# K's inverse norms to rows through DRAM from head 2 on, and K's squares turned inside Q's product

## The reference

```
x = x + pool_mixer(rmsnorm(x));  x = x + mlp(rmsnorm(x))        # layer 0; mlp: square(relu(h @ w_in)) @ w_out, width 4096
kv = rmsnorm(x) @ w_kv                                          # (512, 2048): K for 8 heads x 2 halves of 64, V for 8 heads of 128
k  = rmsnorm(kv[..., :1024] per group of 64) * k_norm
q  = rmsnorm((rmsnorm(x) @ w_q) per group of 64) * q_norm / 8
s  = q @ k.T + bias(distance bucket, head), causal               # two score matrices per head
a  = softmax(s[0]) - lambda * softmax(s[1]);  o = a @ v
x = x + (rmsnorm(o per head) * subln * (1 - lambda_init)) @ w_o;  x = x + mlp(rmsnorm(x))
```

## Time and profile before

| | us |
|---|---|
| median of 3 runs (lowest, highest) | 941.27 (940.96, 941.45) |
| the profiled execution's own time | 941.54 |
| its span | 939.7 |
| PE busy | 934.1 (99%) |
| DVE busy | 683.8 (73%) |
| ACT busy | 470.7 (50%) |
| POOL busy | 89.8 (10%) |
| granted clock of TensorE | 1.0 |

### The profile page before, as it was taken

How to read it: one execution, slowest core, us unless ns; L and a number is a source line. 1 busy time by engine, 2 the same in 40 slices (tenths; PEclk the granted TensorE clock), 3 DMA queues, 4 the chain that set the end, 5 groups by cost and what they waited for, 6 DMA issues and landing times.

```text
span 939.7 us, 11721 instructions
## 1 busy us (share of the span) xinstructions
PE 934.1 (99%) x4439; PEld 771.6 (82%) x4439; DVE 683.8 (73%) x989; ACT 470.7 (50%) x614; POOL 89.8 (10%) x70
## 2 busy tenths in 40 slices
PE   9999999999999999999999999999999999999998
PEld 7888888888888888888888887888888888888887
DVE  6876766676676689988887886757766676667685
ACT  7644343333434438787777773535334333433441
POOL 3000000100000002123222220000100000010010
PEclk9999999999999999999999999999999999999999
DMA  7328682494556644233333232336485458248535
GB/s 258 105 90 239 153 234 90 99 264 129 135 142 173 179 85 120 71 107 93 102 103 103 90 101 90 90 91 188 126 248 155 122 121 250 90 92 225 175 90 135
DMA packets 101583, 130.45 MB, mean 139 GB/s; under 512 B 4297, under 2 KB 63481, under 8 KB 101537
## 3 DMA queue, kind: packets, MB, share of 16 engines
q1 hardware_dynamic: 85632, 98.31, 32.0%
q0 software_dynamic: 14080, 29.91, 17.5%
q10 hardware_dynamic: 1824, 1.61, 0.7%
HBM read 127.69 MB, written 4.75 MB: 141 GB/s over the span
## 4 chain that ended last, share of the span: by engine, by line
PE 91%; DVE 4%; ACT 2%; DMA 2%; issue 1%; SPq 0%; ACTq 0%; DVEq 0%
PE bank L1695 28%; PE bank L1697 28%; PE bank L1696 28%; PE bank L1967 2%; PE bank L1957 1%; DMA raw<-in_w_mlp_out_dram 1%; DVE w_low L1080 1%; PE bank L1996 1%; DMA work<-in_x_dram 1%; PE bank L1872 1%; DVE a_low_buf L1163 0%; ACT w_high L729 0%; ACT w_high L666 0%; PE bank L1938 0%; PE bank L1806 0%
## 5 line engine op out<-in xcount | busy, mean ns | idle before, releaser
L1695 PE MATMUL bank<-h_high_buf,w_high 128*128 128x512 f32 x640 | 252.2, 394 | 0.0
L1697 PE MATMUL bank<-h_high_buf,w_low 128*128 128x512 f32 x640 | 249.5, 390 | 0.0
L1696 PE MATMUL bank<-h_low_buf,w_high 128*128 128x512 f32 x640 | 249.1, 389 | 0.0
L1695 PE MATMUL bank<-w_high,a_high_buf 128*128 128x512 f32 (+1 forms) x452 | 176.1, 390 | 0.1
L1697 PE MATMUL bank<-w_high,a_low_buf 128*128 128x512 f32 (+1 forms) x452 | 175.1, 387 | 0.0
L1696 PE MATMUL bank<-w_low,a_high_buf 128*128 128x512 f32 (+1 forms) x452 | 175.1, 387 | 0.0
L1080 DVE TENSOR_TENSOR w_low<-raw,w_high 128x2048 fp32r<-128x2048 f32 (+2 forms) x56 | 120.3, 2148 | 51.4 <-ACT w_high L729 31.8
L1695 PEld LDWEIGHTS bank<-h_high_buf,w_high 128*128 128x128 f32 x640 | 120.2, 188 | 26.5 <-issue 2.2
L1697 PEld LDWEIGHTS bank<-h_high_buf,w_low 128*128 128x128 f32 x640 | 120.1, 188 | 25.5
L1696 PEld LDWEIGHTS bank<-h_low_buf,w_high 128*128 128x128 f32 x640 | 120.3, 188 | 24.1
L738 ACT ACTIVATE work<-work 128x512 f32<-128x512 f32 x64 | 40.0, 632 | 177.9 <-DVE work L1147 177.9
(11 more groups left out here) (187 smaller groups left out, 1162.5 us busy)
## 6 DMA issues: line engine op xcount, KB each, us to landing
raw<-in_w_mlp_out_dram SPq DMA_DIRECT2D x24, 1024.0 KB, 6.8
raw<-in_w_mlp_out_dram POOLq DMA_DIRECT2D x24, 1024.0 KB, 8.5
raw<-in_w_mlp_in_dram SPq DMA_DIRECT2D x16, 1024.0 KB, 6.2
work<-in_w_mlp_out_dram SPq DMA_DIRECT2D x8, 1024.0 KB, 5.1
work<-in_w_mlp_in_dram SPq DMA_DIRECT2D x8, 1024.0 KB, 7.6
raw<-in_w_kv_dram SPq DMA_DIRECT2D x16, 512.0 KB, 4.0
xT<-in_w_mlp_out_dram SPq DMA_DIRECT2D x8, 1024.0 KB, 4.8
xT<-in_w_mlp_in_dram SPq DMA_DIRECT2D x8, 1024.0 KB, 7.0
```

What stands on the lines that cost most here:

```text
L1695: pe.matmul(acc, w_hi, m_hi, start=start, stop=False, skip_group_check=onto)
L1696: pe.matmul(acc, w_hi, m_lo, start=False, stop=False, skip_group_check=onto)
L1697: return pe.matmul(acc, w_lo, m_hi, start=False, stop=stop, skip_group_check=onto)
```

## The change

From head 2 on (n = 2 to 7, prepared in heads 1 to 6) K's inverse norms no longer pass PE. K's sums get their own eps, root and inverse ahead of Q's (`k_sums`, `k_roots`, `k_inverses`), SP stores them to a DRAM tensor of two rows of 512 and reads each row back into 64 partitions of the buffer of K's squares (`spread_k_rows`), and `k_norm_rows` multiplies K with it at a stride of four. The spread by DVE and the turn by PE go for these heads. SP issues the store and the two loads between its loads of K's and Q's weights and its load of V's. `turn_ksq` moves from behind Q's product to behind five of its eight chunks. POOL waits for `k_inverse` before its K half split. Heads 0 and 1 are normalized as before.

```diff
--- before.py
+++ after.py
@@ -239,6 +239,7 @@
 
         SUM_BANK = [I[0], I[1], I[2], I[3], O[2], O[3], I[1], I[3]]
 
+        k_row = nc.dram_tensor("k_rstd_rows", (2, S), F32, kind="Internal").ap()
         o_row = nc.dram_tensor("o_rstd_row", (S,), F32, kind="Internal").ap()
         scratch_rows = nc.dram_tensor("bias_rows_by_distance", (H, REL), F32, kind="Internal").ap()
         scratch = nc.dram_tensor("bias_by_distance", (H, P, REL), F32, kind="Internal").ap()
@@ -283,6 +284,12 @@
         half_low = sem("half_low")
         pool_low = sem("pool_low")
         w_used = sem("w_used")
+
+        k_total = sem("k_total")
+        k_rooted = sem("k_rooted")
+        k_inverse = sem("k_inverse")
+        k_row_stored = sem("k_row_stored")
+        k_row_landed = sem("k_row_landed")
 
         consts_ready = sem("consts_ready")
         zeros_ready = sem("zeros_ready")
@@ -530,12 +537,32 @@
 
             load_mlp(0)
 
-            with sp.Fori(0, H) as n:
+            def load_kq(n):
                 slot_free(U_HEAD + 2 * n)
                 sp.dma_start(tile3(raw[1][:, 0:1024], KC), wk_v[:, :, bass.ds(n * P, P)]).then_inc(w_landed[1], 16)
                 sp.dma_start(tile3(raw[1][:, 1024:2048], KC), wq_v[:, :, bass.ds(n * P, P)]).then_inc(w_landed[1], 16)
+
+            def load_v(n):
                 slot_free(U_HEAD + 1 + 2 * n)
                 sp.dma_start(tile3(raw[0][:, 0:1024], KC), wk_v[:, :, bass.ds(D + n * P, P)]).then_inc(w_landed[0], 16)
+
+            def spread_k_rows(n):
+
+                sp.wait_ge(k_inverse, n - 1)
+                sp.dma_start(k_row.rearrange("c (p i) -> p c i", p=P), kq_rstd_buf[:, 0:8].rearrange("p (c i) -> p c i", c=2))\
+                  .then_inc(k_row_stored, 16)
+                sp.wait_ge(k_row_stored, 16 * n - 16)
+                sp.wait_ge(kn_ready, n)
+                for c in range(2):
+                    sp.dma_start(ksq[c * HD:(c + 1) * HD, :], k_row[c:c + 1, :].to_broadcast([HD, S])).then_inc(k_row_landed, 16)
+
+            with sp.Fori(0, 3) as n:
+                load_kq(n)
+                load_v(n)
+            with sp.Fori(3, H) as n:
+                load_kq(n)
+                spread_k_rows(n - 1)
+                load_v(n)
             for f in range(NF):
                 for q in range(2):
                     u = U_WO + 2 * f + q
@@ -547,6 +574,8 @@
                     else:
                         sp.dma_start(tile3(raw[u % 2], 4), wo_v[:, 4 * q:4 * q + 4, f * S:(f + 1) * S])\
                           .then_inc(w_landed[u % 2], 16)
+                    if u == U_WO:
+                        spread_k_rows(H - 1)
             load_mlp(1)
 
             for p, half, f in ((P2, 0, 0), (P3, 0, 1), (P7, 1, 1), (P4, 1, 0)):
@@ -647,6 +676,8 @@
                     pool.wait_ge(k_low_done, 1)
                 if h == 1:
                     pool.wait_ge(neg_ready, 2)
+                if h >= 2:
+                    pool.wait_ge(k_inverse, h - 1)
                 if h == H - 1:
                     pool.wait_ge(half_high, h + 1)
                     pool.tensor_tensor(w_low_buf[1][:, 0:UNIT // 2], raw[1][:, 0:UNIT // 2], w_high_buf[1][:, 0:UNIT // 2].bitcast(F32),
@@ -881,6 +912,15 @@
                 act.wait_ge(kq_total, n + 1)
                 act.activation(kq_root_buf[:, :], kq_sum_buf[:, :], ACT.Sqrt, scale=1.0 / HD).then_inc(kq_rooted, 1)
 
+            def k_roots(n):
+
+                act.wait_ge(k_total, n - 1)
+                act.activation(kq_root_buf[:, 0:8], kq_sum_buf[:, 0:8], ACT.Sqrt, scale=1.0 / HD).then_inc(k_rooted, 1)
+
+            def q_roots(n):
+                act.wait_ge(kq_total, n + 1)
+                act.activation(kq_root_buf[:, 8:16], kq_sum_buf[:, 8:16], ACT.Sqrt, scale=1.0 / HD).then_inc(kq_rooted, 1)
+
             def k_high(n):
                 act.wait_ge(kn_ready, n + 1)
                 act.activation(k_hi, kf, ACT.Copy).then_inc(k_high_done, 1)
@@ -1003,6 +1043,7 @@
                 split_v(n)
                 if not second:
                     split_high_first(n + 1, kq_landed(n + 1))
+                k_roots(n)
                 square_q(n)
                 q_high(n)
                 if second:
@@ -1010,7 +1051,7 @@
                 at_highs(h, range(1))
                 if last:
                     o_high(0)
-                kq_roots(n)
+                q_roots(n)
                 o_roots(h - 1)
                 at_highs(h, range(1, 3))
                 bias_scale(n, (0, 1))
@@ -1446,10 +1487,32 @@
                 if first:
                     dve.tensor_tensor(w_low_buf[0][:, 512:1024], raw[0][:, 512:1024], f32(w_high_buf[0][:, 512:1024]), ALU.subtract)\
                        .then_inc(w_low, 1)
-                else:
-                    q_low(n)
                 kq_reduce(n, q_bank, qsq_turned, 1)
                 kq_add_eps(n)
+
+            def k_sums(n, b):
+
+                kq_reduce(n, b, ksq_turned, 0)
+                dve.wait_ge(kq_sum, 2 * n + 1)
+                dve.tensor_tensor(kq_sum_buf[:, 0:8], kq_sum_buf[:, 0:8], kq_eps[:, :], ALU.add).then_inc(k_total, 1)
+
+            def q_sums(n, b):
+
+                kq_reduce(n, b, qsq_turned, 1)
+                dve.wait_ge(kq_sum, 2 * n + 2)
+                dve.tensor_tensor(kq_sum_buf[:, 8:16], kq_sum_buf[:, 8:16], kq_eps[:, :], ALU.add).then_inc(kq_total, 1)
+
+            def k_inverses(n):
+
+                dve.wait_ge(k_rooted, n - 1)
+                dve.reciprocal(kq_rstd_buf[:, 0:8].rearrange("p (c i) -> p i c", c=2), kq_root_buf[:, 0:8].rearrange("p (i c) -> p i c", c=2))\
+                   .then_inc(k_inverse, 1)
+
+            def q_inverses(n):
+                dve.wait_ge(kq_rooted, n + 1)
+                dve.reciprocal(kq_rstd_buf[:, 8:16], kq_root_buf[:, 8:16]).then_inc(kq_inverse, 1)
+                dve.wait_ge(kq_inverse, n + 1)
+                dve.tensor_scalar(neg_rstd_q[:, :], kq_rstd_buf[:, 8:16], -1.0, None, ALU.mult).then_inc(neg_ready, 1)
 
             def half_low_of(n):
                 dve.wait_ge(half_high, n)
@@ -1473,6 +1536,12 @@
             def k_norm(n, b):
                 dve.wait_ge(k_turned, n + 1)
                 dve.tensor_tensor(kf, kf, b[:, :], ALU.mult).then_inc(kn_ready, 1)
+
+            def k_norm_rows(n):
+
+                dve.wait_ge(k_row_landed, 32 * n - 32)
+                k = kf.rearrange("p (i n) -> p i n", i=TT)
+                dve.tensor_tensor(k, k, ksq.rearrange("p (n i) -> p i n", i=TT), ALU.mult).then_inc(kn_ready, 1)
 
             def k_low(n):
                 dve.wait_ge(k_high_done, n + 1)
@@ -1606,15 +1675,24 @@
                 combine(h, 3)
                 if not first:
                     split_low(U_HEAD + 1 + 2 * n, 0, 1024)
+                    k_sums(n, I[0])
                     o_sums(h - 1, I[3])
-                kq_sums(n, I[0], O[3], first)
-                kq_inverses(n)
+                    k_inverses(n)
+                    q_low(n)
+                    q_sums(n, O[3])
+                    q_inverses(n)
+                else:
+                    kq_sums(n, I[0], O[3], first)
+                    kq_inverses(n)
                 if not first:
                     if not second:
                         dve.wait_ge(o_row_stored, 16 * h - 16)
                     o_inverses(h - 1)
                 at_lows(h)
-                k_norm(n, I[0])
+                if first:
+                    k_norm(n, I[0])
+                else:
+                    k_norm_rows(n)
                 if first:
                     q_low(n)
                 else:
@@ -2033,22 +2111,28 @@
                     pe.wait_ge(half_low, n)
                     project(None, 1, 0, I[0], h_high_buf, h_low_buf, k_proj)
                 pe.wait_ge(w_low, U_HEAD + 1 + 2 * n)
-                project(None, 1, 1024, I[1], a_high_buf, a_low_buf, w_used)
+                if first:
+                    project(None, 1, 1024, I[1], a_high_buf, a_low_buf, w_used)
+                else:
+                    project(None, 1, 1024, I[1], a_high_buf, a_low_buf, None, range(0, 5))
+                    turn_ksq(n, I[0])
+                    project(None, 1, 1024, I[1], a_high_buf, a_low_buf, w_used, range(5, KC))
                 pe.wait_ge(v_low, n)
                 if first:
                     pe.wait_ge(second_v_low, 1)
                     project(None, 0, 0, I[2], h_high_buf, h_low_buf, None, range(0, 3))
                 else:
                     pe.wait_ge(w_low, U_HEAD + 2 + 2 * n)
-                if not first:
-                    turn_ksq(n, I[0])
                 turn_probs(h)
                 turn_qsq(n, O[3])
                 if first:
                     pe.wait_ge(w_low, U_HEAD + 2 + 2 * n)
-                project(None, 0, 0, I[2], h_high_buf, h_low_buf, None, range(3, 6) if first else range(0, 5))
-                turn(ksq, I[0], k_spread, n, k_turned)
-                project(None, 0, 0, I[2], h_high_buf, h_low_buf, w_used, range(6 if first else 5, KC))
+                if first:
```

(5 more changed lines are left out.)

## The result

The changed kernel takes 944.94 us (median of six runs, 944.51 to 946.67), the kernel before beside it 941.57 (940.96 to 942.36). The ratio is 1.0037, 95% interval 1.0024 to 1.0050. The forecast was 940.9: the kernel moved the other way. The profiled execution took 944.51 with a span of 942.7, 3.0 us more than before.

The account below looks back on a forecast made before the run. PE, busy 99%, bounds the kernel; its 2.6 us gain shrinks to 1.5 because a loop beside PE lasts 17.45 + 6.76 = 24.21 us. The last section takes 1.05, leaving 0.4: 941.1 profiled, forecast 940.9, range 938.9 to 945.5.

Parts of the forecast that it names:

- PE's side: Four transposes fewer per head save 0.44 us, the moved turn costs nothing: heads of 23.90, 2.6 us over six.
- DVE's side: Copy removed (0.34 us), small K operations added, strided K norm 1.00 instead of 0.60: next P at t + 6.76.
- t: Start of K's norm on DVE in a head; S + 20.50 in the kernel before.
- POOL's wait: POOL's K half starts behind K's inverse (about P + 12.55) and holds Q's add on DVE until P + 15.1.
- P: Start of the first reciprocal of `combine` on DVE in a head; S + 2.51 in the kernel before.
- The trip: K's inverse norms through DRAM, store and two loads: taken as 4.9 us (bounds 4.6 and 6.9), landing at P + 17.45.
- P2: P in head 2; forecast at 3.16 us behind that head's start.
- P7: The P behind head 6, where the loops end; forecast at S + 3.56 from head 4 on.
- (b): Rival: K's store lands late, each us behind P + 17.45 lengthens a head by one; two to four heads, 945; chance 0.30.
- (c): Rival: POOL's Q half comes between two DVE bias operations, PE waits 2 us per head for the scores: 953; chance 0.03.
- S: Start of a head's scores on PE.
- The last section: Section behind the last head follows DVE, so it inherits P: P's move from S + 2.51 to S + 3.56 takes 1.05 us back.

Follow-up runs that it names:

- The run with a trip of 4.83: Changed kernel with each of the two loads of K's rows reading into 16 partitions instead of 64: 941.45 us, ratio 0.9996.
- the fastest kernel: Changed kernel with K's sums and inverse ahead of V's split on DVE, and PE's wait for V's low split moved behind its turns: 940.79 us, ratio 0.9987.

## Why the prediction was wrong

**PE's side: right in the loop.** The turns that go are 0.44 per head; 24.34 became 23.87 where nothing else is late, and the moved turn cost the loop nothing.

**DVE's side: right.** From t to the next P 6.76 in heads 2 to 5 (forecast 6.76); 0.98 for the strided norm (1.00).

**POOL's wait: right.** K's inverse at P + 12.54 (12.55), Q's add takes 0.49 (over 0.4). The lock of the Trainium skill, page "SBUF — State Buffer", section "SBUF: two separate sides", came out as it was weighed there: the add without POOL's wait ends when POOL's split ends.

**The trip: the step that failed.** "I take 4.9" was 5.1 to 6.0, mean 5.51, and DVE idled for the rows in each of heads 2 to 6, which the prediction had named as the sign that it falls. Part of the error was in the adding up, before any run. Store, second issue, load and hand-overs, 1.4 + 0.35 + 3.1 + 0.3, are 5.15 and not 4.9. The lower bound of 4.6 leaves out the second issue, which the upper has (3.7 is 3.3 + 0.35); with it the bound is 4.95, and the value taken lies below. The terms, measured over heads 2 to 6:

| us | forecast | measured, mean | |
|---|---|---|---|
| store, issue to landing | 1.4 | 1.70 | 1.54 or 1.55 in four heads, 2.32 in head 6 |
| second issue | 0.35 | 0.52 | |
| second load, issue to landing | 3.1 | 3.23 | 2.98 to 3.46 |
| hand-overs | 0.3 | 0.07 | |
| sum | 5.15, taken as 4.9 | 5.51 | |

With 5.15 the loop would have been 12.55 + 5.15 + 6.76 = 24.46, more than the 24.34 of the kernel before: by its own terms the change had nothing to win in the loop.

What it cost: P2 to P7 is 124.64, and the forecast's five loops are 121.05. Of these 3.6 us the trips are 5 x 0.61 = 3.0. Another 0.89 is the end of head 6 (7.65 for 6.76), which the kernel before has too and the loop's formula does not, and the earlier inverse in head 6 gives 0.3 back. The run with a trip of 4.83 took 941.45, 3.9 us by the difference of the ratios (1.0037 - 0.9996) below the changed kernel, and its ratio is the forecast one (940.9 for 941.27 is 0.9996). The trip therefore explains most of the miss; the runs scatter too much to divide the rest.

The rival that came true is (b) in its arithmetic and mostly not in its cause. It laid the lateness on the store, in two to four heads; the store was late in head 6 alone, and the rows were late in all five. By the Trainium skill, page "DMA: Bandwidth & Descriptors", section "Anatomy of one DMA — SWDGE (gpsimd) path", the store was about 2.0, the trip 5.5 and the sum 944.5, close to the 5.51 and the 944.94. The store itself measured 1.54 in four heads of five, so that sum was near by luck. The chance for a time over 943.2, 0.30, is that of (b) alone; with (c) it is 0.33.

**Heads 1 and 2: a second error.** A gain of 0.44 in each was forecast from head 4's offsets. Head 1 is written out in another order: its Q add took 1.64 before and takes 2.10 after. In the kernel before with the moved turn alone it takes 2.03, and the head is 0.54 longer, so in this head the move was not free, as the prediction had taken it. K's norm starts right behind `at_lows`, PE waits 0.23 for the low parts of the attention weights and 0.34 for `k_low`, and nothing of PE's turn is left (24.80 for 24.74). P2 is at S + 3.77 instead of the 3.16 forecast. In head 2 PE waits 0.78 for ACT's squares of O. Both heads stay long (24.78 and 24.76) where the trip is short; the wait for ACT is 0.77 there, and 0.77 in the fastest kernel too.

**The last section: right.** P7 is at S + 4.45 instead of 3.41: 1.04 (forecast 1.05). It is measured against S; P7 to the end did not change. In the fastest kernel, too, the section takes 1.0 of the heads' gain back (P7 at S + 4.44), although P is only at S + 3.08 in its head 6. The trace shows most of the cause: in that head DVE waits 0.66 for the rows, behind a store of 2.76:

```profile
541.40 2.76 DMA k_rstd_rows<-kq_rstd_buf
544.18 0.45 SPq L557
544.67 3.09 DMA work<-k_rstd_rows
```

In every kernel whose loads wait for the store, the store of head 6 is late: 2.3 to 2.8 from its issue to that of the first load, where heads 2 to 5 have 1.6. It is the head in which SP loads the weights of the output product. What makes that store late was not tested.

**Not foreseen: PE's two other waits.** The turn of O's squares waits for ACT (1.7 us in all), and V's low split stands in front of PE's turns. The kernel before has neither wait. The second appeared only when K's sums had been moved ahead of V's split: the loop got shorter, and the wait hid that from the time.

## What to carry to other kernels

A hand-off moved from a busy engine to a queue takes its place in a loop through all the engines: write down that loop's period, add up every term of the trip, and take the latest landing the rows allow beside the median, for each us over is paid in every turn of it. Here the medians alone, added up, gave a loop longer than the head it was to shorten. When the loop binds, start the trip earlier before trying to shorten it, and then look for the waits that stand in a program earlier than their first use: with K's inverse 0.9 us earlier in the loop (P + 11.6 for 12.54) the kernel took 944.8, as much as the changed one, and with PE's wait for V's split moved as well 940.8 (the first of the two also held V's load back). Count a written-out first or last iteration by its own rows, not by those of the loop.

## What the runs showed of the hardware

- The same 256 KB in two loads of 64 partitions each lands 3.3 us (median) behind each issue; in one load with an outer size of 2 it drew 48 GB/s at a DMA share of 0.13, and the trip took 4.9 us more.
- Loads of that shape from a row of an input, issued 0.6 us behind the store, took 4.4 us, and from the row just stored, behind its landing, 3.3. Which of the two differences makes it is open.
- A quarter of the bytes in as many DMAs: 2.4 instead of 3.3 to landing. Taken as linear in the bytes, some 2.1 of the 3.3 are not bytes (an estimate from these two values).
- The 4 KB store landed in 1.54 or 1.55 in heads 2 to 5 and in 2.32 in head 6 of the same execution.
- A VectorE add of 128 x 8 with two SBUF operands takes 0.17, and 1.61 when POOL's split of 128 x 1024 is under way, until that split ends. The other way round, POOL's split takes 3.27 instead of 2.39 when DVE's split of V's weights has started 0.2 before it (the fastest kernel).
- A float32 multiplication of 128 x 512 on VectorE takes 0.98 from start to start with one operand at a stride of four elements, and 0.61 at a stride of one.
- After PE had stood idle for 4.4 us, the granted clock was 0.89 over the head (one load for two), so a stretch of it ran at 1.2 instead of 2.4 GHz. With V's load after the norm, head 2 had waits of 1.16 and 0.78 us, a mean clock of 0.93 and took 26.09; in the changed kernel the same two waits were 0.34 and 0.78, and the clock was 1.00:

```profile
431.71:457.80 26.09, 25.30 (x135) 20.95 (x136) 20.09 (x57) 19.48 (x43) 5.75 (x4) 0.93 0.41 113
```
